# Output projection by halves over three tiles, an opening with products of zeros, channel sums on VectorE, a first group that opens its banks, and an exponent moved

## What is computed

```python
for l in range(2):
    hn = rmsnorm(x, ln_mix[l])
    x = x + (even_mixer(hn) if l == 0 else gla_mixer(hn))       # each ends in "... @ w_out"
    x = x + peer(rmsnorm(x, ln_ffn[l]))
return rmsnorm(x, ln_final)

# even_mixer: q, k, v, glu = split(h @ w_in)
#   a = differential attention (4 heads, T5 bias), RMS per head
#   c = silu(layernorm(depthwise conv, width 31, of c_val * sigmoid(c_gate)))   # 512 channels
#   return concat(a, c) @ w_out
# peer: queries -> scores against 2 x 128 keys -> top 16 of each -> top 16 of the sums
#   gate = softmax(top values); act = gelu(expert_u @ x); out = sum(gate * act * expert_v)
```

## Time and profile before

| | us |
|---|---|
| median of 3 runs | 2885.51 (2883.32 to 2887.55) |
| the profiled execution | 2887.83 |
| its span, first to last instruction | 2886.0 |
| TensorE busy in the span | 2844.4 (99%), 14647 products |
| VectorE busy | 2275.9 (79%) |
| ScalarE busy | 1016.5 (35%) |
| GpSimd busy | 747.3 (26%) |
| mean granted clock of TensorE | 0.996 of 2.4 GHz |

### The profile page before, as it was taken

How to read it: one execution, slowest core, us unless ns; L and a number is a source line. 1 busy time by engine, 2 the same in 40 slices (tenths; PEclk the granted TensorE clock), 3 DMA queues, 4 the chain that set the end, 5 groups by cost and what they waited for, 6 DMA issues and landing times.

```text
span 2886.0 us, 39729 instructions
## 1 busy us (share of the span) xinstructions
PE 2844.4 (99%) x14647; PEld 1530.7 (53%) x14716; DVE 2275.9 (79%) x4294; ACT 1016.5 (35%) x1347; POOL 747.3 (26%) x518
## 2 busy tenths in 40 slices
PE   8999999999999999999999899999999999999998
PEld 4455555556666444444544455555566664444443
DVE  6854899987888899999501248999968888999996
ACT  2163322334555333333321233232345553333332
POOL 0000233321111554544000001333211114454450
PEclk9999999999999999999999999999999999999999
DMA  4213677767998999999221236777669989999993
GB/s 155 88 46 140 233 276 283 293 247 255 310 311 291 392 396 396 398 399 396 105 88 59 75 115 223 271 301 275 257 247 313 311 284 400 389 400 396 397 397 146
DMA packets 210562, 775.96 MB, mean 269 GB/s; under 512 B 15461, under 2 KB 97513, under 8 KB 190345
## 3 DMA queue, kind: packets, MB, share of 16 engines
q1 hardware_dynamic: 45824, 416.87, 37.8%
q0 software_dynamic: 73728, 268.47, 25.0%
q10 hardware_dynamic: 90888, 89.14, 9.1%
HBM read 681.88 MB, written 92.54 MB: 268 GB/s over the span
## 4 chain that ended last, share of the span: by engine, by line
PE 93%; issue 2%; ACT 1%; DVE 1%; DMA 1%; PEld 1%; DVEq 0%; PEldq 0%; ACTq 0%; SPq 0%
PE ps L1721 32%; PE ps L1648 11%; PE ps L1649 11%; PE ps L1650 11%; PE ps L1622 8%; PE ps L1341 5%; PE ps L1332 4%; PE ps L1361 4%; PE ps L1701 2%; PE ps L1700 2%; PE ps L1658 1%; PEld ps L1721 1%; DMA arena<-in_u 1%; PE ps L1427 1%; PE ps L1509 0%
## 5 line engine op out<-in xcount | busy, mean ns | idle before, releaser
L1721 PE MATMUL ps<-arena 128*128 128x512 bf16 x4541 | 992.2, 379 | 3.9 <-issue 0.2
L476 POOL DMA_INDIRECT arena<-in_ur,arena x256 | 348.9, 1363 | 1614.8 <-DVE arena L1055 936.3
L1721 PEld LDWEIGHTS ps<-arena 128*128 128x128 bf16 x4608 | 450.6, 98 | 544.6 <-issue 2.3
L1028 DVE TENSOR_TENSOR arena<-arena 128x1024 bf16<-128x1024 f32 x512 | 611.9, 1221 | 123.9 <-ACT arena L693 100.4
L1648 PE MATMUL ps<-xnh,arena 128*128 128x384 bf16 x2048 | 668.5, 326 | 5.3 <-ACT arena L719 5.3
L1650 PE MATMUL ps<-xnh,arena 128*128 128x384 bf16 x2048 | 668.8, 327 | 0.0
L1649 PE MATMUL ps<-xnl,arena 128*128 128x384 bf16 x2048 | 668.8, 327 | 0.0
L693 ACT ACTIVATE arena<-arena 128x1024 bf16<-128x1024 f32 x512 | 524.8, 1048 | 146.5 <-PE ps L1721 107.3
L476 POOL DMA_INDIRECT arena<-in_v,arena x256 | 397.4, 1552 | 405.8 <-DVE x_res L1064 342.9
L1064 DVE SCALAR_TENSOR_TENSOR x_res<-arena,x_res 128x1024 f32<-128x1024 f32 x256 | 328.6, 1283 | 21.1 <-issue 0.9
L719 ACT ACTIVATE arena<-ps 128x384 f32<-128x384 f32 x256 | 125.5, 490 | 556.2 <-PE ps L1650 541.8
(11 more groups left out here) (198 smaller groups left out, 2274.9 us busy)
## 6 DMA issues: line engine op xcount, KB each, us to landing
arena<-in_v SPq DMA_DIRECT2D x64, 2048.0 KB
arena<-in_u SPq DMA_DIRECT2D x62, 2048.0 KB
h_scratch<-arena ACTq DMA_DIRECT2D x60, 768.0 KB
arena<-h_scratch SPq DMA_DIRECT2D x60, 768.0 KB
arena<-gate_scratch SPq DMA_DIRECT2D x64, 640.0 KB
arena<-in_wmix SPq DMA_DIRECT2D x15, 2048.0 KB, 8.0
gate_scratch<-xnT ACTq DMA_DIRECT2D x10, 2048.0 KB
gate_scratch<-arena ACTq DMA_DIRECT2D x10, 2048.0 KB
```

The costliest lines, as they stand in the source:

```text
L476: pool.indirect_dma_start(ring[n % NBUF], None, ur_d[L] if g < P else vr_d[L], at).then_inc(gat_in[n % NBUF], 16)
L1028: dve.tensor_tensor(lo[:, s], raw[s // TPG][:, s % TPG], hi[:, s], ALU.subtract).then_inc(lo_ready, 1)
L1721: last = pe.matmul(ps[:, 2 + 2 * tt + dh], c, v[:, TPG * s + q, dh * 512:(dh + 1) * 512], start=False, stop=stop and c is cl)
```

## The change

- `project_out` follows a list of steps. In layer 1 it takes the first column half of token tiles 0, 1 and 2, then the second half of the same, then tile 3; it waits for a weight block only where the block is first used; the last head transposes come behind the first step. In layer 0 the order stays.
- The opening: constants in two loads (identity and ones first), the selector after x, the first weight block in two interleaved halves of 1 MB, ACT waits for its primers later and takes a Sqrt of a constant first, PE runs 14 + 3 + 1 products of zeros around the transposes of tiles 0 to 2, the setup products come behind these and go to banks 2 and 3, and the first two units are done by token halves: half of unit 0, transposes of tile 3, half of unit 1, then both second halves.
- The sums over channel tiles go from PE to DVE: three adds, then one product against ones, for the mean and again for the squares. `conv_done` is given after the logits of units 0 and 1 and three adds. PE does four slices of the v projection ahead of it where there were two.
- The six products of zeros ahead of the `v` groups go; the first product of each bank opens it, for which the first two groups stand in front of the loop.
- The exponent of the gates goes two tiles earlier on ACT. On DVE six `dots` go ahead of the wait for it, with one more `ahead`.

The diff, cut to its core:

```diff
@@ SP
             x_load(0)
-            sp.dma_start(const[:], const_d).then_inc(consts_in, 16)
-            sp.dma_start(cols[:], cols_d).then_inc(consts_in, 16)
-            sp.dma_start(relb[:], relb_d).then_inc(consts_in, 16)
+            sp.dma_start(const[:, 0:K_IOTA], const_d[:, 0:K_IOTA]).then_inc(ident_in, 16)
+            sp.dma_start(cols[:], cols_d).then_inc(cols_in, 16)
             x_load(1)
-            sp.dma_start(m_hot[0:32], hot_d).then_inc(hot_in, 16)
+            sp.dma_start(relb[:], relb_d).then_inc(relb_in, 16)
             x_load(2)
             x_load(3)
+            sp.dma_start(m_hot[0:32], hot_d).then_inc(hot_in, 16)
+            def first_load():
+                pairs = [w.rearrange("p k (a c) -> p (k a) c", c=2 * P) for w in (wblk[0], wmix_d[0])]
+                sp.dma_start(pairs[0][:, :, 0:P], pairs[1][:, :, 0:P]).then_inc(w_first, 16)
+                sp.dma_start(pairs[0][:, :, P:], pairs[1][:, :, P:]).then_inc(w_in[0], 16)
+                sp.dma_start(const[:, K_IOTA:], const_d[:, K_IOTA:]).then_inc(rest_in, 16)
@@ ACT, mixer0
+                act.activation(std[:, 0:1], epsc[:], ACT.Sqrt)
                 for tt in range(3):
                     norm_tile(0, tt)
-                act.wait_ge(consts_in, CONST_DMAS)
+                act.wait_ge(cols_in, 16)
                 norm_low(0, 0)
+                norm_low(0, 1)
                 norm_tile(0, 3)
@@ ACT, the squares ahead of the copy of v
                     if u == 1:
-                        unit_out(m_v[:, 0])
                         for ct in range(CT):
                             act.wait_ge(yc_ready, ct + 1)
                             act.activation(m_sq[:, ct], m_y[:, ct], ACT.Square).then_inc(sq_ready, 1)
+                        unit_out(m_v[:, 0])
@@ ACT, peer
-                    if n == NK // 2 + 6:
+                    if n == NK // 2 + 4:
                         act.wait_ge(ge_sub, L + 1)
                         act.activation(ex, ex, ACT.Exp).then_inc(ge_exp, 1)
@@ DVE, mixer0
                 logits(0)
                 logits(1)
+                dve.tensor_tensor(m_sig[:, 0], m_y[:, 0], m_y[:, 1], ALU.add)
+                dve.tensor_tensor(m_sig[:, 1], m_y[:, 2], m_y[:, 3], ALU.add)
+                dve.drain()
+                dve.tensor_tensor(m_sig[:, 0], m_sig[:, 0], m_sig[:, 1], ALU.add).then_inc(conv_done, 1)
...
+                    if u == 1:
+                        for pair in range(2):
+                            dve.wait_ge(sq_ready, 2 * pair + 2)
+                            dve.tensor_tensor(m_sig[:, 2 + pair], m_sq[:, 2 * pair], m_sq[:, 2 * pair + 1], ALU.add)
+                        dve.drain()
+                        dve.tensor_tensor(m_sig[:, 2], m_sig[:, 2], m_sig[:, 3], ALU.add).then_inc(sq_sum, 1)
@@ DVE, peer
-                for n in range(6, 10):
+                for n in range(6, 11):
                     ahead(NK // 2 + n)
+                    if n < 9:
+                        dots(2)
                 dve.wait_ge(ge_exp, L + 1)
...
-                for n in range(10, 13):
+                for n in range(11, 13):
                     ahead(NK // 2 + n)
-                    dots(2)
@@ the order of the output projection
+        out_steps = [[(tt, dh) for tt in range(TT) for dh in range(2)],
+                     [(0, 0), (1, 0), (2, 0), (0, 1), (1, 1), (2, 1), (3, 0), (3, 1)]]
+        after = [1, 0]
@@ PE, mixer0
+                pe.wait_ge(zeros_ready, 1)
+                idle_products(14)
+                pe.wait_ge(ident_in, 16)
+                turned(0, 0)
+                idle_products(3)
+                turned(0, 1)
+                idle_products(1)
+                turned(0, 2)
...                # setup products, now to banks 2 and 3
+                pe.wait_ge(w_first, 16)
+                pe.wait_ge(xt_low, 2)
+                pe.wait_ge(xt_high, 2)
+                banks = unit_bank(), unit_bank()
+                first_half(banks[0], 0, slice(0, T // 2))
+                turned(0, 3)
+                first_half(banks[1], 2, slice(0, T // 2))
                 all_turned(0)
-                pe.wait_ge(tab_ready, 1)
+                for bank, c in zip(banks, (0, 2)):
+                    first_half(bank, c, slice(T // 2, T)).then_inc(p_done, 1)
...
-                v_part(v_bank, 0, 0, 2)
-
+                v_part(v_bank, 0, 0, 4)
                 pe.wait_ge(conv_done, 1)
-                for ct in range(CT):
-                    last = pe.matmul(ps[:, 7], ones, m_y[:, ct], start=ct == 0, stop=ct == CT - 1)
-                last.then_inc(st_done, 1)
+                pe.matmul(ps[:, 7], ones, m_sig[:, 0], start=True, stop=True).then_inc(st_done, 1)
@@ PE, peer
-                for b in range(2, 8):
-                    pe.matmul(ps[:, b], zeros[:, 0:P], zeros[:], start=True, stop=False)
...
-                with pe.Fori(0, NG // 2 - 1) as i:
+                group(0, 0, True)
+                group(0, 1)
+                with pe.Fori(1, NG // 2 - 1) as i:
```

More of the change, by code:

```diff
@@ L433, in peer_loads @@
                         sp.dma_start(hsf[s], h_d[i * 2 + s]).then_inc(gh_in[s], 16)
-            for b in range(2):
-                block_load(b)
+            first_load()
+            block_load(1)
             sp.wait_ge(tab_ready, 1)
@@ L494, in _ @@
                 act.dma_start(prime[2 + s:3 + s], const_d[s:s + 1, 0:P]).then_inc(g_out[s], 16)
-            for s in range(2):
-                act.wait_ge(h_out[s], 16)
-                act.wait_ge(g_out[s], 16)
             def norm_tile(k, tt):
@@ L859, in mixer0 @@
+                norm_high(0, 1)
+                norm_tile(0, 3)
+                dve.wait_ge(setup_mm, 2)
+                dve.tensor_copy(m_tab, ps[:, 2:4].rearrange("p a b -> p (a b)")[:, 0:REL]).then_inc(tab_ready, 1)
+                for tt in range(2, TT):
                     norm_high(0, tt)
+                dve.wait_ge(rest_in, 16)
+                dve.tensor_copy(iota_2[:], iota.unsqueeze(2).to_broadcast([P, P, 2]))
                 dve.wait_ge(pool_prep, 1)
@@ L1344, in project_out @@
             def project_out(m, b0, src, order, between, begun=0):
[L1346 to L1367 removed]
+                seen = [False, False]
@@ new lines, in project_out @@
+                for step, (tt, dh) in enumerate(out_steps[m]):
+                    b = b0 + dh
+                    if not seen[dh]:
+                        arrived(b)
+                        seen[dh] = True
+                    j = outs[0]
+                    outs[0] += 1
+                    if j >= 2:
+                        pe.wait_ge(o_free, j - 1)
+                    at = slice(tt * P, (tt + 1) * P)
+                    for n, (kd, done, count) in enumerate(order):
+                        if tt == 0 and n < begun:
+                            continue
+                        if dh == 0 and count[tt]:
+                            pe.wait_ge(done, count[tt])
+                        last = pe.matmul(ps[:, j % 2], src[:, kd, at], wblk[b % 2][:, kd], start=n == 0, stop=n == KD - 1)
+                    last.then_inc(o_done, 1)
+                    if step and out_steps[m][step - 1][1] == 1:
+                        pt = out_steps[m][step - 1][0]
+                        if pt == 0:
+                            pe.wait_ge(tr_free, HEADS + 2 * TT * m)
+                        turned(2 * m + 1, pt)
+                    if step == after[m]:
@@ L1368, in project_out, with idle_products @@
                         between()
             def mixer0():
+                def idle_products(count):
+                    for _ in range(count):
+                        pe.matmul(ps[:, 1], zeros[:, 0:P], zeros[:], start=True, stop=True)
+                pe.wait_ge(zeros_ready, 1)
[6 more added lines that the diff above has]
+                turned(0, 2)
@@ new lines, in mixer0, with first_half @@
+                pe.matmul(ps[:, 3, 0:REL - 512], relb8[:].rearrange("p h j -> p (h j)"), m_hot[0:32, 512:REL], start=True, stop=True).then_inc(setup_mm, 1)
+                def first_half(bank, c, at):
+                    for kd in range(KD):
+                        last = pe.matmul(bank[:, at], wblk[0][:, kd, c * P:(c + 1) * P], xnT[:, kd, at],
+                                         start=kd == 0, stop=kd == KD - 1)
+                    return last
+                pe.wait_ge(w_first, 16)
@@ L1385, in mixer0 @@
+                for c in (0, 2, 1, 3):
+                    by_columns(1, c)
                 for b in range(2, 4):
@@ L1464, in mixer0 @@
                         bank = unit_bank()
-                        for ct in range(CT):
-                            pe.wait_ge(sq_ready, ct + 1)
-                            last = pe.matmul(bank, ones, m_sq[:, ct], start=ct == 0, stop=ct == CT - 1)
-                        last.then_inc(p_done, 1)
+                        pe.wait_ge(sq_sum, 1)
+                        pe.matmul(bank, ones, m_sig[:, 2], start=True, stop=True).then_inc(p_done, 1)
                     if u == 2:
```

(3 more changed lines are left out.)

119 lines of the change are left out of this document (48 added, 71 removed).

## The result

| | median of runs, us | profiled execution, us | its span, us |
|---|---|---|---|
| kernel before | 2884.41 (2880.75 to 2887.55, 4 runs) | 2887.83 | 2886.0 |
| changed kernel | 2859.41 (2857.37 to 2861.39, 4 runs) | 2859.40 | 2857.6 |

The ratio is 0.9914, 95% interval 0.9897 to 0.9931. The medians stand 25.0 us apart, the two profiled executions 28.4 us; most of that difference is explained under `before_again`. The forecast was 2855.3, the range 2849 to 2866.

The account below looks back on a forecast made before the run. TensorE, working in 99% of the span, was taken as the bound. Terms 11.2 + 8.1 + 4.7 + 3.6 + 2.6 = 30.2 us took 2887.83 to 2857.6, less 2.3 for the median: 2855.3 us, range 2849 to 2866.

Parts of the forecast that it names:

- Output projection of layer 1: New order there removes a 7.5 us weight wait, 2.1 of slow clock and 1.6 of VectorE wait: 11.2 us.
- The norm of tile 2: In layer 1's output projection, it has 7.9 us and needs 7.0, so it holds by 0.9.
- The exponent of the gates: Both layers, `u` tiles: an earlier exponent and load remove 5.3 us of stalls and 2.8 of clock loss, 8.1 us.
- The rival of a stall that stays: At the gates, loads only change places and ScalarE still waits: 2863.4 us, chance 0.11.
- the 2.3: Microseconds by which the earlier kernel's median lay below its profiled execution, subtracted from 2857.6 to give 2855.3.
- the zeros of `v`: Removing the products of zeros ahead of the `v` groups saves 1.3 us in each layer, 2.6 us.
- The channel sums: In attention, moving the adds from TensorE to VectorE saves 4.7 us, bounds 1.5 and 5.2.
- The opening: Start of the kernel: input projection starts at 14.7, two units done at 29.3 instead of 33.0; gain 3.6 us.
- no bound: In the opening, the first weights arrive by 14.4 us at the latest, so they do not delay the 14.7 start.
- the rival of a fallen clock: The opening gives nothing because TensorE's clock falls back or weight pieces come late: 2858.9 us, chance 0.13.
- the forecast's own signs of being wrong: Clock below 2.4 GHz behind 14 us, VectorE's first gate after 30.3, or ScalarE over 4 us at `in_u`, Gelu queued.
- nothing waits behind them that isn't ready: At the start of the `v` groups, removing the zero products exposes no late input, so 2.6 us is saved.

Follow-up runs that it names:

- before_again: The kernel before, unchanged, run again for a second trace and more times; 2885.39 us.
- e2: The kernel before with only the new order of layer 1's output projection; 2872.99 us, ratio 0.9959.
- e3: The kernel before with 34 products of zeros ahead of the weight-block wait of layer 1's output projection, the wait kept; 2882.63 us, ratio 0.9991.
- e5: The kernel before with only ScalarE's half of the gates edit, the exponent two tiles earlier; 2881.46 us, ratio 0.9987.
- e6: The kernel before with only VectorE's half of the gates edit, six dots and one more split ahead of the wait; 2881.48 us, ratio 0.9985.
- after: The changed kernel with all edits, as profiled and, where two are counted, traced again; median 2859.41 us, ratio 0.9914.
- e1: The changed kernel with the six products of zeros back ahead of the v groups and the loop over all groups; 2859.65 us, ratio 0.9918.
- e7: The changed kernel with both channel sums back on TensorE as four products against ones each; 2864.87 us, ratio 0.9934.
- e8: The changed kernel with VectorE's dots of the first four v groups spread 3, 2, 5, 5 instead of 3, 4, 4, 4; 2858.32 us, ratio 0.9912.
- e9: The changed kernel with three products of zeros ahead of each of two 0.8 us waits in layer 1's mixer; 2860.34 us, ratio 0.991.
- e10: The changed kernel with later VectorE dots, zeros ahead of two mixer waits, and input projection started before tile 2's transposes and the setup products; 2859.26 us, ratio 0.9909.
- after_again: The changed kernel, unchanged, run again for a second trace and more times; 2859.07 us, ratio 0.9909.
- e4: The changed kernel without the 18 products of zeros in its opening; 2861.65 us, ratio 0.9921.

## Why the prediction was right, point by point

**The total.** Forecast 2855.3, median 2859.4; for the pair of profiled executions 30.2 us were forecast and 28.4 came. Between the medians it is 25.0. Four of the five mechanisms did what was said of them. What is missing comes from a term that brought nothing and from one that was sized from a single execution.

**Output projection of layer 1.** 11.2 forecast, 11.5 in the traces, 12.4 between medians (e2). Its parts hold too: the wait is gone, the clock's part is 2.0 by e3 where 2.1 was forecast. The norm of tile 2, the step with the least room (0.9 us), caused no wait.

**The exponent of the gates.** Forecast 8.1, and 4.4 + 4.3 = 8.6 in the first pair of traces. The load was to go 11 us earlier: it goes at 647.46, where stages before it have gained 8.32, so 11.3 earlier. It lands 11.4 us later, with 3.8 to spare. The rival of a stall that stays did not come in any of eight traces of the changed code. What failed is the step from the profiled execution to the median: the whole 8.1 was taken off the profiled time, and then the 2.3 by which the median lies lower was taken off as well. The stall is not a constant of the kernel. Its mean is 5.5 in four traces, and 3.9 is what e5 and e6 saved, so the profiled execution had some 3 us of stall more than a typical one, which is an estimate of what the 2.3 was. For the median the term is 2.6 too large, as much as the zeros of `v`. These two are the gap between 30.2 and 25.0; the other terms together came out 0.6 better than forecast, and 0.6 is left unexplained.

**The channel sums.** 4.7 forecast, 4.5 measured, with the wait at the second sum at 1.26 where 1.4 was forecast.

**The opening.** 3.6 forecast, 3.8 in the first pair. That the weights are "no bound" held by little: the half block issued at 4.51 took 9.8 us and landed at 14.29, 0.1 ahead of the start, which the setup products set. The forecast gave the rival of a fallen clock 0.13; of seven traces with this opening (two of after, e1, e7, e8, e9, and e10 up to tile 1) the clock fell in two. In those two the forecast's own signs of being wrong came: a clock below 2.4 GHz behind 14 us, and VectorE's first gate later than 30.3. That the first pair agrees with the forecast so well is in part luck, since neither of its two executions had the fall. On average the term is 4.1, because the old opening has the fall too.

**The zeros of `v`.** 2.6 forecast, nothing came: in the first pair 0.2 in layer 0, and in layer 1 0.2 ahead of the first `v` product (4.5 less the 4.3 of the gates) and -0.5 in the products, so 0 within 0.1. This is the term that was mis-sized, and the step that failed is "nothing waits behind them that isn't ready". The first two groups were ready. The third was not, since it needs VectorE, which had used these 1.3 us; and in layer 1 another 0.85 goes to a wait with no releaser, whose cause stays open. The forecast looked at the first instruction behind the removed work, not at the first that needs another engine.

**The sum for typical executions.** Opening 4.1 (mean start of attention 130.97 in six traces with the opening of before, 126.83 in six with that of after), attention 4.5, gates 5.5, output projection 11.5, zeros about 0: 25.6, against 25.0 between the medians.

## What to carry to other kernels

Before a stall is priced, look whether it has the same depth in every place and execution with the same code; if it ends with a transfer, its depth in one trace is one draw, and the part that an edit saves is the mean. Where work is taken out ahead of a loop, follow every engine that feeds the loop to the first iteration in which it was just in time, not only to the first instruction. An earlier start is worth what is taken off the engine's path, so work that fills a wait must be counted when it is moved out of it.

## What the runs showed of the hardware

- **The same opening, with the clock held in four traces and lost in two.** In the six traces of the full opening the 14 products of zeros took 5.4 to 6.0 us in four (after, e1, e7, e8) and 4.66 and 4.62 in two (after_again, e9): the clock had risen earlier within them (their records shorten at 4.4 us in after_again, at 6.1 in after), so they ended sooner, and TensorE then stood 1.26 and 1.19 us for the first tile instead of 0 to 0.7. Only in those two did the clock fall at about 15 us, at a cost of 1.6 and 1.5 us. All six had the same transposes, so these don't decide it; the idle time differs, but that it is the cause is not shown. More than 14 such products would be the test, and it wasn't made. The Trainium skill (TensorE: Matmul & The Clock Gate, Part 4: PE-mode transpose) says that transposes don't count as busy for the clock in the same way. The traces neither need that rule for this fall nor refute it, and no run here took the transposes away. They don't agree on the rise either: in the kernel before it came at 14.7 us in a run of transposes, 6.4 us after the setup products had begun; in e4 TensorE worked with hardly a gap from 10.6 us, first on transposes, then on setup products and the half unit, and the rise came only at 22.9.
- **The same fall, two sizes.** The mixer of layer 1, up to its head transposes, took 192.6 us once (e4), 194.3 nine times and 196.0 four times: steps of 1.7 us, by how long the clock is down. e9 and e10 have six products of zeros more there; the other twelve traces have the same instructions.
- **One load, 9.9 to 12.5 us.** The same load, beside the same six gathers, took so long from issue to use in the two layers of four traces with one code, and 8.1 and 8.7 where the gathers went first (e6), while the 383 us of the `u` stream ahead of it repeated within 0.01 us in all fourteen traces.
